# The mixer of a two-layer block in another order: query panels earlier, convolution taps later, attention's output panels among the heads

## What is computed

```python
h = rms_norm(x, mix_norm[l])
p = h @ w_in[l]                       # 384 query latent, 256 key/value latent, 32 rope, 2 x 512 convolution
attn = mla_group(...)                 # q = norm(c_q) @ w_uq, k, v = norm(c_kv) @ w_ukv, 8 heads,
                                      # per-head rms norms, rope, chunk-causal softmax, P @ v
conv = conv_group(p[..., o_cv:], conv_w[l], conv_b[l], conv_ln_g[l], conv_ln_b[l])
x = x + jnp.concatenate([attn, conv], axis=-1) @ w_out[l]

def conv_group(u_raw, conv_w, conv_b, ln_g, ln_b):
    a, g = u_raw[..., :CONV_W], u_raw[..., CONV_W:]
    u = a * jax.nn.sigmoid(g)
    y = lax.conv_general_dilated(u, ...)     # 31 taps back in time, each channel by itself
    return jax.nn.silu(layer_norm(y + conv_b, ln_g, ln_b))
```

## Time and profile before

| | |
|---|---|
| median of 3 executions | 2332.32 us |
| lowest, highest | 2327.3, 2332.44 us |
| profiled execution, and its span | 2332.38 us, 2330.7 us |
| PE busy | 2268.5 us (97%) |
| DVE busy | 1605.5 us (69%) |
| ACT busy | 1102.0 us (47%) |
| mean granted TensorE clock | 0.992 of 2.4 GHz |
| mixer of layer 0, first input panel to last output panel | 135.35 us |
| mixer of layer 1, the same | 130.61 us |

### The profile page before, as it was taken

The page is one execution under the profiler, slowest core; times in us unless marked ns, Lnnn a source line. Parts: engine busy times, 40 slices in busy tenths (PEclk is TensorE's granted clock), DMA queues, the critical chain, the costliest instruction groups (busy, mean ns, idle before and its releaser), DMA issues.

```text
span 2330.7 us, 37481 instructions
## 1 busy us (share of the span) xinstructions
PE 2268.5 (97%) x13900; PEld 1973.0 (85%) x13900; DVE 1605.5 (69%) x2706; ACT 1102.0 (47%) x1748; POOL 112.1 (5%) x155
## 2 busy tenths in 40 slices
PE   9999999999999989999999999999999999999998
PEld 8998779998998779997777778888888888888888
DVE  6677857667667957777455554444546999988896
ACT  5443444445343354435555543334434666565664
POOL 0000000000000001112121201001000000000000
PEclk9999999999999999999999998999999999999999
DMA  8655126655564226664343521221221222222222
GB/s 328 228 199 181 64 100 245 232 205 200 208 230 166 82 100 217 228 222 82 73 71 74 72 99 64 73 73 64 73 82 64 91 90 81 81 81 90 81 99 91
DMA packets 83068, 301.88 MB, mean 130 GB/s; under 512 B 10404, under 2 KB 10788, under 8 KB 82468
## 3 DMA queue, kind: packets, MB, share of 16 engines
q1 hardware_dynamic: 78336, 284.72, 35.0%
q0 software_dynamic: 2048, 4.20, 3.2%
q10 hardware_dynamic: 2600, 11.81, 1.4%
HBM read 299.64 MB, written 1.05 MB: 129 GB/s over the span
## 4 chain that ended last, share of the span: by engine, by line
PE 78%; DVE 15%; ACT 4%; issue 3%; DVEq 0%; DMA 0%; ACTq 0%; another core or an unknown queue 0%
PE ps L749 49%; PE ps L797 12%; PE ps L861 4%; DVE wsplit L2158 3%; DVE work L2875 2%; PE ps L1365 2%; DVE work L2887 2%; PE ps L1226 1%; PE ps L1089 1%; PE ps L1103 1%; PE ps L764 1%; PE ps L1079 1%; DVE work L2907 1%; DVE work L2919 1%; ACT wsplit L1493 1%
## 5 line engine op out<-in xcount | busy, mean ns | idle before, releaser
L749 PE MATMUL ps<-hsplit,wsplit 128*128 128x256 f32 (+1 forms) x8376 | 1380.3, 322 | 26.8 <-DVE wsplit L2158 11.5
L749 PEld LDWEIGHTS ps<-hsplit,wsplit 128*128 128x128 f32 x8376 | 1205.6, 191 | 159.3 <-DVE wsplit L2158 18.4
L2158 DVE TENSOR_TENSOR wsplit<-ring,wsplit 128x1024 fp32r<-128x1024 f32 x465 | 576.3, 1241 | 344.4 <-ACT wsplit L1493 342.4
L1493 ACT ACTIVATE wsplit<-ring 128x1024 fp32r<-128x1024 f32 x463 | 488.6, 1058 | 514.5 <-PE ps L749 394.6
L797 PE MATMUL ps<-wsplit,fsplit 128*128 128x512 f32 x1056 | 256.5, 392 | 1.9 <-DVE fsplit L2292 1.7
L797 PEld LDWEIGHTS ps<-wsplit,fsplit 128*128 128x128 f32 x1056 | 192.6, 188 | 40.1 <-issue 3.3
L2254 DVE SCALAR_TENSOR_TENSOR work<-ring,work 128x1024 f32<-128x1024 f32 x96 | 120.3, 1253 | 1.1 <-DMA ring<-panels 1.1
L1573 ACT ACTIVATE work<-ps 128x256 f32<-128x256 f32 x88 | 33.8, 384 | 161.0 <-PE ps L749 161.0
L2378 DVE SCALAR_TENSOR_TENSOR work<-work,vec 128x256 f32<-128x256 f32 x240 | 100.9, 481 | 1.7
L749 PEld LDWEIGHTS ps<-wsplit,hsplit 128*128 128x128 f32 x768 | 96.0, 198 | 5.3 <-issue 3.8
L861 PE MATMUL ps<-work,ring 128*128 128x256 f32 x416 | 99.2, 387 | 0.0
(11 more groups left out here) (369 smaller groups left out, 2307.6 us busy)
## 6 DMA issues: line engine op xcount, KB each, us to landing
ring<-panels SPq DMA_DIRECT2D x539, 512.0 KB, 4.1
work<-latent_weights ACTq DMA_DIRECT2D x2, 2304.0 KB, 11.9
work<-rpb POOLq DMA_DIRECT2D x64, 64.0 KB, 6.6
work<-conditions ACTq DMA_DIRECT2D x6, 512.0 KB, 7.0
cst<-constants ACTq DMA_DIRECT2D x1, 1408.0 KB
work<-x SPq DMA_DIRECT2D x2, 512.0 KB, 4.8
work<-post_rows ACTq DMA_DIRECT2D x2, 512.0 KB, 4.0
cT<-ctx ACTq DMA_DIRECT2D x1, 1024.0 KB, 7.3
```

Of the source, the lines that this page charges most:

```text
L749: ins = mm(out_, w(a), x(b), start=start and n == 0, stop=stop and n == 2, **kw)
L1493: af(wsplit[:, split_slot(name, n), 0, :], ring[:, slot, :], ACT.Copy).then_inc(high_ready, 1)
L2158: tt(parts[:, 1, :], ring[:, slot, :], parts[:, 0, :].bitcast(fp32), ALU.subtract)\
```

## The change

The host packs the query panels ahead of convolution groups 2 and 3, and `w_out` in its own order, attention's four panels first. PE's projections follow: panels 6 to 8 are the query latent, 9 and 10 are group 2, and 11 and 12, group 3, stand after the values and between the two `turn_heads`. The sums of the convolution's norm move behind the sixth head (`conv_sum`) and behind the loop (`conv_var`). Attention's output is turned pair by pair (`turn_out`) in the loop. On DVE, groups 0 and 1 are finished first, then group 2 has 10 taps ahead of the head norms and 12 between their pieces, and its last 9 and all 31 of group 3 stand in the head loop, up to 6 of each per head. ACT computes the convolution's silu by its own function instead of by exponentials, which takes two loads of function tables per layer. `keep_clock` counts are smaller. The core of the diff:

```diff
 PE
+                win(6, 3, 0, between=lambda j: rope(j))
+                win(7, 3, 1, between=lambda j: rope(4 + j))
+                pe.wait_ge(lat_ready, l * 2 + 1)
+                win(8, 4, 0, between=lambda j: latent_sum(j // 2, 0, j % 2))
                 pe.wait_ge(conv_u_ready, l * 4 + 1)
+                win(9, 0, 0, between=lambda j: rope(8 + j))
+                win(10, 0, 1, between=lambda j: rope(12 + j))
...
-                pe.wait_ge(v_ready, l * 2 + 2)
-                keep_clock(1, 20)
-                pe.wait_ge(conv_sq_ready, l + 1)
...
-                keep_clock(1, 12)
+                pe.wait_ge(conv_u_ready, l * 4 + 3)
+                win(11, 0, 0)
                 turn_heads(0)
+                win(12, 0, 1)
                 turn_heads(1)
+                keep_clock(2, 10)
...
+                def turn_out(m):
+                    pe.wait_ge(attn_ready, l * 4 + m + 1)
+                    for t in range(2):
+                        last = nc.tensor.transpose(ps[:, OUT_BANK[m], t * 128:(t + 1) * 128],
+                                                   o_tok[:, t, m * 128:(m + 1) * 128], cst[:, K_ID:K_ID + 128])
+                    last.then_inc(attn_turned, 1)
+                def conv_sum():
+                    pe.wait_ge(conv_acc_ready, l * 4 + 4)
+                    for c in range(4):
+                        last = mm(ps[:, 4, 0:T], ones[:, :], acc[:, c, :], start=c == 0, stop=c == 3)
+                    last.then_inc(conv_sum_done, 1)
...
                 for h in range(HEADS):
                     if h < 3:
-                        keep_clock(1, 15 if h == 0 else 2)
+                        keep_clock(2, 12 if h == 0 else 2)
+                    if h in (4, 6):
+                        pe.wait_ge(mix_split_ready, l * 6 + h // 2)
                     transposes(h)
                     if h + 2 < HEADS:
                         scores(h + 2)
+                    if h == 2:
+                        turn_out(0)
                     values(h)
                     if h in (3, 5):
-                        wout(h // 2 - 1)
-                wout(2)
...
+                        wout(h // 2 - 1, (0,))
+                        turn_out(h // 2)
+                        wout(h // 2 - 1, (1,))
+                    if h == 6:
+                        conv_sum()
+                conv_var()
+                wout(2, (0,))
+                turn_out(3)
+                wout(2, (1,))
 ACT
+                squares(0)
+                act.wait_ge(tok_ready, l * 2 + 2)
+                head_factors(0)
+                squares(1)
+                values_out(0)
+                head_factors(1)
+                values_out(1)
+                for n in range(3):
+                    high("wout", l, n)
                 heads_in(0)
+                gate(3)
                 heads_in(1)
...
+                for h in range(4):
                     exps(h)
+                out_high(0)
+                exps(4)
+                exps(5)
+                out_high(1)
                 high("wout", l, 3)
+                exps(6)
+                exps(7)
+                out_high(2)
+                high("wout", l, 4)
+                act.wait_ge(conv_centred, l + 1)
+                af(conv_sq, gate_x, ACT.Square).then_inc(conv_sq_ready, 1)
...
+                act.wait_ge(conv_rstd_ready, l + 1)
+                nc.scalar.preload_act_table_set("silu_and_others")
+                out_high(3)
+                for p in range(2):
+                    act.wait_ge(conv_dve_stage, l * 2 + p + 1)
+                    for c in (2 * p, 2 * p + 1):
+                        A.did(af(mix[:, 4 + c, :], acc[:, c, :], ACT.Silu, scale=..., bias=...))
+                    A.need()
+                    af(hsplit[:, 0, 4 + 2 * p:6 + 2 * p, :], mix[:, 4 + 2 * p:6 + 2 * p, :], ACT.Copy).then_inc(mix_high, 1)
+                nc.scalar.preload_act_table_set("natural_log_exp_and_others")
+                for n in range(5, 8):
                     high("wout", l, n)
 DVE
                 gate_in(0)
                 gated(0)
+                taps(0, 10)
+                gate_in(1)
+                taps(0, 3)
+                gated(1)
+                taps(0, 1)
+                for j in range(CONV_K):
+                    taps(0, 1)
+                    taps(1, 1)
+                    if j == 3:
+                        ada_out(l, 0)
+                gate_in(2)
+                gated(2)
+                taps(2, 10)
...
                 mean_squares(0)
...
+                taps(2, 2)
                 turned_heads(0)
+                mean_squares(1)
+                taps(2, 2)
+                turned_heads(1)
+                taps(2, 6)
+                gate_in(3)
+                taps(2, 2)
+                gated(3)
                 low("wout", l, 0)
...
                     if h + 2 < HEADS:
                         maxima(h + 2)
                     if h == 2:
+                        out_low(0)
+                    if h < 2:
+                        low("wout", l, h + 1)
+                    for _ in range(6):
+                        taps(2, 1)
+                        taps(3, 1)
+                    if h == 7:
+                        dve.wait_ge(conv_sum_done, l + 1)
+                        stt(gate_x, wide(ps[:, 4, 0:T], 4), -1.0 / CONV_W, acc[:, :, :], ALU.mult, ALU.add)
...
+                    if h in (3, 5):
+                        out_low(h // 2)
+                        low("wout", l, h // 2 + 2)
```

More of the change, by code:

```diff
@@ L912, in values_in @@
                 def values_in(t):
[L914 removed]
+                    pe.wait_ge(*((conv_u_ready, l * 4 + 2) if t == 0 else (v_ready, l * 2 + 1)))
                     for k in range(2):
@@ L1658, in mixer, with squares @@
                 af(lat_s2, lat_l, ACT.Exp, scale=-1.0).then_inc(tok_ready, 1)
-                for t in range(2):
+                def squares(t):
                     act.wait_ge(head_proj_done, l * 2 + t + 1)
@@ L1666, in mixer, with head_factors @@
                     af(k_sq[t], ps[:, 6 + t, :].rearrange("p (h c) -> p h c", h=HEADS), ACT.Square).then_inc(head_sq, 1)
-                    if t == 0:
-                        act.wait_ge(tok_ready, l * 2 + 2)
-                    else:
-                        high("wout", l, 0)
-                    act.wait_ge(v_proj_done, l * 2 + t + 1)
-                    af(vsb[:, t, :], ps[:, 1, :], ACT.Copy, scale=lat_s[:, t:t + 1]).then_inc(v_ready, 1)
-                high("wout", l, 1)
-                high("wout", l, 2)
-                for t in range(2):
+                def head_factors(t):
                     act.wait_ge(head_ms, l * 2 + t + 1)
@@ L2382, in tap, with taps @@
                         last_tap[c] = V.did(ins)
[L2384 to L2385 removed]
+                next_tap = [0] * 4
+                def taps(c, count):
+                    for _ in range(count):
+                        if next_tap[c] < CONV_K:
+                            tap(c, next_tap[c])
+                            next_tap[c] += 1
                 gate_in(0)
                 gated(0)
[L2388 to L2407 removed]
+                taps(0, 10)
[11 more added lines that the diff above has]
+                taps(2, 10)
                 dve.wait_ge(tok_ready, l * 2 + 2)
```

165 lines of the change are left out of this document (51 added, 114 removed).

## The result

The changed kernel takes **2366.73 us** (median of 4 executions, 2366.24 to 2366.85), the kernel before 2332.35 us on the same chip: ratio 1.0152, 95% interval 1.0135 to 1.0170, slower by 34.4 us. The forecast was 2360, with a stated range of 2346 to 2374; the time also lies 0.7 us above the narrower range of the forecast's own case, 2354 to 2366.

A forecast was written before the change was run, and what follows sets the result against it. DVE, busy 98.88 of 130.61 us, and its in-order queue between probability copies set the pace. Layer 1 +12.5 and layer 0 +7.8 give +20.3, clock +8, on 2332.4: 2360 us, range 2346 to 2374.

The forecast's parts named there:

- the forecast's own case: Whole kernel: clock falls in the head loop, costing 4 us a layer; 2360 us, own range 2354 to 2366, chance 0.50.
- to the first copy: Mixer start to first probability copy, per layer: first transposes at 813.2 against 826.36, 13.2 us earlier.
- Projections: PE's input panels: two panels' worth (6.95 us) moves behind head projections, a 0.84 us wait goes; they start at 778.6.
- Head norms: Between head projections and scores: gate round trips, taps and ACT's queue give back part of the gain.
- The rival of later heads (2368): Ahead of the scores: gate 3 on ACT and DVE makes heads 4 us later, +8; 2368 us, chance 0.05.
- Head loop: First to last probability copy: taps and chains in DVE's order make it 41.8 us, 21.4 us more a layer.
- Tail: Last copy to end of last output panel: 23.7 us against 19.3, 4.3 us more a layer.
- Table load: ACT's function table loads in the tail: 1.28 us each; by the skill's 2.66 the sum would be 2366.
- Clock: PE's gaps in the head loop lower its clock: 4 us a layer, +8, between bounds 0 and 8.2 a layer.
- the rival at 2369: Head loop: PE at half clock through the whole loop, adding 16.4 us; 2369 us, chance 0.17.
- the rival at 2352.7: Head loop: full clock throughout, no clock loss; 2352.7 us, chance 0.22.
- Packed taps: Head loop: taps pack into DVE's idle time, copies under 4.2 us apart; not slower, some 2328 us, chance 0.06.

The follow-up runs named there:

- filled kernel: Changed kernel plus matmuls that compute nothing (or add zeros) in PE's waits of the head loop; 2357.22 us, ratio 1.0111.
- run without taps: Changed kernel with the convolution's taps in the head loop left out (38 of 124 a layer), so part isn't computed; 2334.18 us, ratio 1.0015.
- kernel with the late table load: Changed kernel with only the second table load moved on ACT behind the high halves of output panels 5 to 7; 2365.40 us, ratio 1.0150.
- hybrid: Mixed order: input panels and all taps ahead of head norms as before, attention's output panels in the loop, silu by function; 2312.87 us, ratio 0.9917.

## Why the prediction was right, and by how much each term was off

The filled kernel gives each term at full clock, and the median of the changed kernel the clock's part.

| term, per layer | forecast | measured | over both layers |
|---|---|---|---|
| to the first copy | -13.2 | -10.7 | +5.0 |
| loop | +21.4 | +21.0 | -0.8 |
| tail | +4.3 | +4.8 | +1.0 |
| clock | +4 | +4.75 | +1.5 |

The last column is measured minus forecast. It adds to 6.7 us, which looks like 2366.7 - 2360, but that match is partly luck: the forecast's own sum, 2332.4 + 20.3 + 8, is 2360.7, so only 6.0 us are to be explained, and the other 0.7 is of the size of the scatter between runs.

- **Projections.** Right: head projections begin 42.53 us after the first panel (793.47 - 750.94); the forecast's 778.6 is 42.6 after its start. DVE waited 4.75 us for panel 10, forecast 4.7.
- **Head norms.** The step that was mis-sized, 2.6 us a layer on the scores (75.64 against 73.0), and the largest error. PE's wait before the second values was 1.07, forecast 1.3. But I took ACT's queue from `values_out` straight to gate 3 and `heads_in(1)`, and passed over `high` 1 and 2, whose count waits for the very panels that were moved. "Now ACT's queue decides" was the right sentence with two instructions missing from it. With them moved, scores come at 72.79, the forecast's 73.0. The rival of later heads (2368) came true in part, but not by gate 3, which it named.
- **Head loop.** Right head by head: 7.0, 6.6, 4.4, 8.8, 4.0, 6.9, 3.6 at full clock against 7.1, 6.8, 4.5, 8.9, 4.15, 6.8, 3.55. The run without taps shows that the taps are most of the loss, and that the chains of heads 3 and 5 are real without them. One sign was off: PE's waits for the copy were to be some 20 us a layer and are 26.2 over both layers, 13.1 each.
- **Tail.** Half a us short. Attention's last low half ends 7.95 us after the last copy (886.68 in layer 1), forecast 8.0; silu and its high halves then took ACT 4.0 us instead of 3.4, and everything after is that much later. The 1.4 us wait before wout 5 measured 1.47.
- **Table load.** In this trace again 1.28 us, with the next ACT instruction 0.02 behind:

```profile
884.54 1.28 ACT L1751 ACT_TABLE_LOAD   x1
885.84 0.39 ACT L1731 ACTIVATE hsplit<-ps 128x256 fp32r<-128x256 f32 x1
```

  The Trainium skill's 2.66 us (ScalarE: Activation LUTs, What ACT_TABLE_LOAD costs) would have put 1.4 us of idle there; the measurement decides for 1.28. That the forecast's sum by that figure, 2366, is nearer to the measured time than 2360 is chance: the idle isn't in the trace, and the missing time is in the terms above.
- **Clock.** The middle case, as chosen: it fell, came back in head 4, and fell again. The size, 4 us a layer, was about the middle of its bounds (0 and 8.2) and not derived, so that 4.75 came so near is partly luck. The loop did not run low throughout, which was the rival at 2369; by time alone 2366.7 is nearer to that rival, and it is the stretches at 1.00 (828 to 838 and 858 to 862) that decide against it. Full clock, the rival at 2352.7, needed empty matmuls. The Trainium skill (TensorE: Matmul & The Clock Gate, HAM oscillation — how this bites in real kernels) says that short bursts between idle times are throttled each time anew; the trace agrees in part, with two such falls in layer 1's loop and a stretch at 1.00 between them.
- **Packed taps.** Refuted. It was to decide at 4.2 us between copies; they are 5.9 apart at full clock (41.3 over 7 gaps).

How much of layer 0's first-copy time in before was clock (94.11 against 90.93) was taken from layer 1 and not tested by itself.

## What to carry to other kernels

Idle time of an engine inside a loop of short hand-overs is not room for work: what stands in front of the instruction that another engine waits for lengthens the loop by nearly its full length (here 15 of 18 us), and only what ends before that input is there is free. When panels are moved in one queue, look in every other queue for instructions that count these panels, see what stands behind them, and ask whether the wait is for the data or only for the count. And when gains are measured one at a time under a clock that falls, repeat them together: the clock added to one of them (7.4 us for some 5.2) and hid another (1.3 for 2.8), and a filler sized for one order can outlast the shorter wait of the next.

## What was not expected of the hardware

- The clock's loss differs between executions of one program: the kernel with the late table load took 2359.08 us at a mean granted clock of 0.986 and 2365.2 to 2366.6 at 0.980 to 0.982. It differs between layers too: the two mixers of before, the same instructions, are 4.7 us apart.
- In the hybrid PE had gaps of 0.55 to 0.74 us before the values and the granted clock was 0.63 in 828 to 832; with the gaps filled it stayed at 1.00 there.
- The changed order with empty matmuls added had PE busy 7.6 us more in layer 0's mixer (135.80 against 128.16), and that mixer was 4.3 us shorter.
